# Rotary columns and the first branch's gate computed channel by token in a hybrid attention kernel

## The chip, the cores and the metric

The kernel runs on one core of a Trainium2 chip. The time is device microseconds of one execution: 505.21 us as the median of three (505.19 to 505.41). The profiled execution took 505.35 us; its span from the first to the last instruction is 503.6 us, and TensorE's granted clock was 0.998 of full speed over it.

## The reference, cut to what matters

One layer on 512 tokens of width 1024, in float32. All projections come from one matrix product of the normalised input:

```python
h = rmsnorm(x, norm_g)
(a_q, a_k, a_v, a_z, i_q, i_k, i_w, b_q, b_k, b_v, b_z, b_o, b_i, b_f, g_a, g_b) = split(h @ w_in)
q_a, k_a = rope(a_q), rope(a_k)             # 8 heads of 64; the first 16 of a head are rotated
q_i, k_i = rope(i_q), rope(i_k)             # 16 indexer heads of 64, one key head
score = sum_h w_i[h] * relu(q_i[h] @ k_i / 8)       # chunk-causal; the best 128 keys of each query stay
o_a = softmax(q_a @ k_a / 8 over those keys) @ v_a
y_a = (o_a * silu(a_z)) @ w_branch_a
q_b, k_b = silu(causal_conv(b_q, b_k))      # 4 taps, 4 heads of 128
cell = mlstm(q_b, k_b, b_v, log_i, log_f)
y_b = (head_norm(sigmoid(b_o) * cell) * silu(b_z)) @ w_branch_b
x = x + (sigmoid(g_a) * y_a + sigmoid(g_b) * y_b) @ w_out
return rmsnorm(x, final_norm_g)
```

The rotation takes partner channels c and c+8 of a head's first 16: x1*cos - x2*sin and x1*sin + x2*cos.

## The kernel before

Every large product is made of three matmuls of rounded parts: each operand is split into a rounded part (hi) and a remainder (lo), and hi*hi, hi*lo and lo*hi are added in PSUM (`three`, L1483). A weight slot holds 1024 columns; SP loads it into one of three raw buffers, ScalarE rounds it (`round_slot`, L868), POOL makes the remainder (`remainder`, L522), and seven split slots are kept.

TensorE's programme is written out by hand. It goes through UNITS: one small unit (indexer key, weights and gate logits), then the groups iq0, iq1, aq, ak, bq, bk, bv, av, bo, bz, az of 512 columns each. A unit is one PSUM bank (`pj`, two of them in turn) of 128 by 512, made of 24 matmuls in four quarters of six. Groups bq and bk have the weight columns as the stationary operand and so come out channel by token, with one unit for 128 channels; all others come out token by channel, with one unit for 128 tokens. iq0 and iq1 have three units each, since the first 128 tokens need no scores. After UNITS come eight rounds c, each with two gate units (g_a and g_b) and two branch products, and then the output projection.

Between the quarters stand side jobs, put at a place by `plan` (L112): place p is quarter p % 4 of unit p // 4. Every engine walks the same places and does its part of the job in order, so an engine that waits in one job holds back all that it has in later places. A job's PSUM comes from one of three rings of two banks (`tr`, `qb`, `ob`). The jobs that matter here:

- stage_chan (14 of them): a unit of iq0, iq1, aq or ak is copied by ScalarE to `stage`, VectorE rotates it with three operations on 128 columns (`rotate_from_bank`, L1135), TensorE turns it channel by token with four transposes, and ScalarE and VectorE split it into iq_parts or k_parts (aq goes to q_a unsplit).
- gate_rows, gate_cols: the mLSTM's gate logs are turned into rows, scanned, and turned back.
- score (48): two matmuls of a head's queries with the indexer keys, relu by ScalarE to `ob`, weighted sum by VectorE. The order is all heads of tokens 384 to 511, then 256 to 383, then 128 to 255.
- the top-k rounds (`round_plan`, L201): 16 rounds for each of three score blocks of 512, 384 and 256 columns, on VectorE alone.
- out_a_chan (4): the unit's gate tanh(a_z/2)+1 times a_z, multiplied with the inverse softmax sums (L1408), is turned by four transposes and multiplied into the attention output o_at (L1332), which is then split into oa_hi (L973) and oa_lo (L1345).

For bq and bk VectorE does the convolution from the unit's bank (`conv`, L1228) in three operations; TensorE may write that bank again, two units later, when the last of them is done (`wait_unit_read`, L578).

## Time and profile before

| | us |
|---|---|
| median of three runs | 505.21 |
| profiled execution | 505.35 |
| its span | 503.6 |
| TensorE busy | 494.5 (98%) |
| VectorE busy | 261.4 (52%) |
| ScalarE busy | 239.2 (47%) |
| POOL busy | 213.0 (42%) |

A busy TensorE counts matmuls that overlap: a row's duration of one matmul is longer than its distance from the next, so distances between starts are what a count of matmuls is multiplied with. Where the page gives a row of digits, each digit is a fortieth of the span, 12.6 us, in tenths of busy time. "Line engine" groups name what an operation writes and reads; `tr<-ident,stage` is a transpose.

### The profile page before, as it was taken

Reading aid. Unit: us, or ns where it says so; the run is one execution under the profiler, and the core shown is the slowest. Engines: PE = TensorE matmul, PEld = TensorE weight load, DVE = VectorE, ACT = ScalarE, POOL = GpSimd, SP = SyncE. Lnnn points to the kernel's source line nnn. Section 1 sums busy time; section 2 is a strip of 40 time slices with the busy share of each in tenths; the row PEclk is TensorE's granted clock in tenths of the full one; section 3 lists DMA queues with packets and bytes.
Section 4 is the critical chain, followed back from the end, with each engine's and each line's share of the span. In section 5 each row is a group of like instructions: output and inputs, shape, how many; then the busy total and the mean of one; then the engine's idle time right before and its main releaser. Section 6 shows DMA issues by size and latency. Waiting matters only on the chain.

```text
span 503.6 us, 6823 instructions
## 1 busy us (share of the span) xinstructions
PE 494.5 (98%) x2518; PEld 411.6 (82%) x2518; DVE 261.4 (52%) x575; ACT 239.2 (47%) x434; POOL 213.0 (42%) x130
## 2 busy tenths in 40 slices
PE   8999999999999999999999999999999999999995
PEld 7688888888888888888788888888888888887885
DVE  3865777877899936525655567531111011125433
ACT  6757655555554455536568652413330333152322
POOL 0675131333344444247487451246534663373000
PEclk9999999999999999999999999999999999999999
DMA  8654432212343243112223112043234426453111
GB/s 284 188 153 128 126 87 79 84 48 80 83 111 99 85 117 104 52 43 85 57 70 85 43 43 65 20 125 104 62 87 125 126 58 193 126 149 144 42 55 72
DMA packets 44841, 48.94 MB, mean 97 GB/s; under 512 B 4996, under 2 KB 30212, under 8 KB 44808
## 3 DMA queue, kind: packets, MB, share of 16 engines
q1 hardware_dynamic: 43944, 47.65, 32.3%
q10 hardware_dynamic: 864, 0.86, 0.5%
q8 instruction: 20, 0.33, 0.3%
q14 instruction: 13, 0.11, 0.1%
HBM read 46.40 MB, written 2.11 MB: 96 GB/s over the span
## 4 chain that ended last, share of the span: by engine, by line
PE 94%; DMA 2%; SPq 1%; POOL 1%; ACT 1%; DVE 1%; issue 1%; DVEq 0%
PE pj L1486 24%; PE pj L1487 24%; PE pj L1488 24%; DMA w_raw<-in_w_in 2%; PE ob L1617 2%; PE tr L1606 2%; PE qb L1554 2%; PE qb L1553 2%; PE ob L1487 1%; PE qb L1487 1%; PE ob L1488 1%; PE qb L1488 1%; PE ob L1486 1%; PE qb L1486 1%; PE tr L1541 1%; PE qb L1601 1%
## 5 line engine op out<-in xcount | busy, mean ns | idle before, releaser
L529 POOL TENSOR_TENSOR w_lo<-w_raw,w_hi 128x1024 fp32r<-128x1024 f32 x70 | 168.9, 2424 | 156.3 <-ACT w_hi L875 156.0
L1486 PE MATMUL pj<-w_hi,h_hi 128*128 128x512 f32 x272 | 109.6, 403 | 0.0
L1488 PE MATMUL pj<-w_hi,h_lo 128*128 128x512 f32 x272 | 106.5, 392 | 0.0
L1487 PE MATMUL pj<-w_lo,h_hi 128*128 128x512 f32 x272 | 106.4, 391 | 0.0
L1486 PE MATMUL pj<-h_hi,w_hi 128*128 128x512 f32 (+1 forms) x200 | 78.1, 390 | 1.0 <-DVE h_lo L1129 1.0
L875 ACT ACTIVATE w_hi<-w_raw 128x1024 fp32r<-128x1024 f32 (+1 forms) x72 | 73.5, 1045 | 9.8 <-DMA w_raw<-in_w_out 6.3
L1488 PE MATMUL pj<-h_hi,w_lo 128*128 128x512 f32 (+1 forms) x200 | 77.9, 389 | 0.0
L1487 PE MATMUL pj<-h_lo,w_hi 128*128 128x512 f32 (+1 forms) x200 | 77.8, 389 | 0.0
L1488 PEld LDWEIGHTS pj<-w_hi,h_lo 128*128 128x128 f32 x272 | 51.1, 188 | 11.4
L1486 PEld LDWEIGHTS pj<-w_hi,h_hi 128*128 128x128 f32 x272 | 51.2, 188 | 8.3 <-issue 0.2
L1487 PEld LDWEIGHTS pj<-w_lo,h_hi 128*128 128x128 f32 x272 | 51.3, 188 | 8.0
L1443 DVE TENSOR_TENSOR prod<-qb,sig 128x512 f32<-128x512 f32 x8 | 5.5, 690 | 77.2 <-PE qb L1488 77.2
L1486 PEld LDWEIGHTS pj<-h_hi,w_hi 128*128 128x128 f32 (+1 forms) x200 | 37.3, 186 | 9.4 <-issue 1.3
L1488 PEld LDWEIGHTS pj<-h_hi,w_lo 128*128 128x128 f32 (+1 forms) x200 | 37.3, 186 | 8.1
L1487 PEld LDWEIGHTS pj<-h_lo,w_hi 128*128 128x128 f32 (+1 forms) x200 | 37.3, 186 | 7.8
L840 POOL TENSOR_TENSOR m_lo<-prod,m_hi 128x512 fp32r<-128x512 f32 x8 | 10.6, 1330 | 60.5 <-ACT m_hi L1088 60.5
L1211 DVE SCALAR_TENSOR_TENSOR score<-ob,idx_w,score 128x512 f32<-128x512 f32 (+2 forms) x45 | 27.7, 616 | 11.5 <-ACT ob L921 8.8
L921 ACT ACTIVATE ob<-qb 128x512 f32<-128x512 f32 (+2 forms) x48 | 22.0, 476 | 16.7 <-PE qb L1554 11.7
L966 ACT ACTIVATE probs<-probs,neg_max 128x128 f32<-128x128 f32 (+3 forms) x32 | 18.0, 562 | 23.3 <-DVE neg_max L1306 23.1
L1088 ACT ACTIVATE m_hi<-prod 128x512 fp32r<-128x512 f32 x8 | 5.1, 632 | 47.3 <-DVE prod L1446 47.3
L1315 DVE COPY probs_t<-tr 128x128 f32<-128x128 f32 (+3 forms) x32 | 15.6, 489 | 22.6 <-PE tr L1606 22.6
L1223 DVE MAX8 top<-score 128x8 f32<-128x512 f32 (+2 forms) x48 | 26.7, 556 | 0.9
(216 smaller groups left out, 817.3 us busy)
## 6 DMA issues: line engine op xcount, KB each, us to landing
w_raw<-in_w_in SPq DMA_DIRECT2D x60, 512.0 KB, 3.6
w_raw<-in_w_out SPq DMA_DIRECT2D x5, 512.0 KB, 3.5
x_tok<-in_x SPq DMA_DIRECT2D x4, 512.0 KB, 5.3
w_raw<-in_w_branch_a SPq DMA_DIRECT2D x8, 256.0 KB, 2.9
w_raw<-in_w_branch_b SPq DMA_DIRECT2D x8, 256.0 KB, 3.3
x_again<-in_x SPq DMA_DIRECT2D x1, 2048.0 KB, 9.3
w_late<-in_w_out SPq DMA_DIRECT2D x3, 512.0 KB, 6.1
out<-y_norm SPq DMA_DIRECT2D x4, 320.0 KB, 2.3
```

Of the source, the lines that this page charges most:

```text
L529: eng.tensor_tensor(lo[:, 0:m], raw_slot(n)[:, 0:m], hi[:, 0:m].bitcast(F32), ALU.subtract).then_inc(lo_by_dve if n in DVE_SLOTS else lo_b ...
L840: pool.tensor_tensor(m_lo[:, c, :], prod[:, c % 2, 0, :], m_hi[:, c, :].bitcast(F32), ALU.subtract)\
L875: act.activation(split_slot(n)[0][:, 0:m], raw_slot(n)[:, 0:m], ACT.Copy).then_inc(hi_made, 1)
L921: act.activation(ob[s % RELUS][:, 0:w], bank_of(job)[:, 0:w], ACT.Relu, scale=float(IDX_DIM) ** -0.5).then_inc(relu_made, 1)
L966: act.activation(probs[:, s % 2, 0:w], probs[:, s % 2, 0:w], ACT.Exp, scale=-1.0, bias=neg_max[:, s:s + 1], accum_out=p_sum[:, s:s + 1])\
L1211: ins = dve.scalar_tensor_tensor(out=acc, in0=ob[s % RELUS][:, 0:w], scalar=wt, in1=acc, op0=ALU.mult, op1=ALU.add)
L1223: link(dve.max(top8[:, i, :], acc))
L1315: dve.tensor_copy(probs_t[:, s % QUAD, 0:w], bank_of(job)[:, 0:w]).then_inc(probs_t_made, 1)
L1486: pe.matmul(bank, a_hi, b_hi, start=first, stop=False)
L1487: pe.matmul(bank, a_hi, b_lo, start=False, stop=False)
L1488: return pe.matmul(bank, a_lo, b_hi, start=False, stop=last)
L1553: pe.matmul(bank[:, 0:w], queries, ik_hi[:, 0:w], start=True, stop=False)
```

## The change

Groups iq0, iq1, aq, ak and az now come out channel by token, like bq and bk: one unit for 128 channels and all tokens. iq0 and iq1 have four units each, with 384 columns (tokens 128 to 511). The transposes of stage_chan and out_a_chan are gone.

The rotation now has its partner in another row. When a group of four units is complete, ScalarE issues four transfers that copy rows 8 to 15 to rows 0 to 7 and back, for both heads of a block, into `swapped` ("swap"). POOL multiplies each block of `swapped` with the sines ("sin"), VectorE multiplies the block with the cosines and adds ("turn"), and ScalarE and VectorE split it ("parts"). The tables cos_t and sin_t, channel by token, are blank from memsets on POOL at the start and filled in the rotated rows by four ScalarE copies in gate_rows, whose four transposes now carry both gate logs and both tables. gate_cols has four transposes too.

Scores go head by head over the three token blocks, since a unit now carries all tokens of two heads, and start eight quarters after iq1 begins. The top-k rounds all start after the last score, one step of 4.5 quarters for a round of each block.

For az, the inverse softmax sums are taken in one operation after the last head ("recip"), turned by one transpose ("sums_chan"), copied, written to a scratch in HBM by a ScalarE transfer, and spread from there over the partitions by two SP transfers into rec_all. Four jobs "gate_a" scale the gate, multiply it into o_at, and split; the last two stand after the az units.

```diff
-UNITS = [("small", 0)] + [(g, j) for g in GROUPS for j in ((3, 2, 1) if g in ("iq0", "iq1") else range(TILES))]
+TURNED = ("iq0", "iq1", "aq", "ak")
+UNITS = [("small", 0)] + [(g, j) for g in GROUPS for j in range(TILES)]
...
-SCORES = [(i, h) for i in (3, 2, 1) for h in range(IDX_HEADS)]
+SCORES = [(i, h) for h in range(IDX_HEADS) for i in (3, 2, 1)]
...
 def score_place(s):
-    return first_quarter("iq1") + 4 + (4 * s) // 5
+    return first_quarter("iq1") + 8 + (4 * s) // 5
...
-    for n, u in enumerate(STAGED):
-        put(4 * UNIT[u] + 4 + 2, "stage_chan", n)
+    for n, g in enumerate(TURNED):
+        end = first[g] + 16
+        put(end, "swap", n)
+        for b in range(KW):
+            put(end + 4 + 3 * b, "sin", 4 * n + b)
+            put(end + 5 + 3 * b, "turn", 4 * n + b)
+            if (g, b) in PARTS:
+                put(end + 6 + 3 * b, "parts", PARTS.index((g, b)))
...
-        if j < TILES - 1:
-            put(first["az"] + 4 * j + 6, "out_a_chan", j)
+    put(first["az"] + 8, "recip")
+    put(first["az"] + 10, "sums_chan")
+    put(first["az"] + 14, "gate_a", 0)
+    put(first["az"] + 15, "gate_a", 1)
...
 def round_plan():
     at = {}
-    start = score_place(IDX_HEADS - 1) + 1
-    place = start
+    start = score_place(len(SCORES) - 1) + 1
     for r in range(ROUNDS):
+        place = start + (9 * r) // 2
         at.setdefault(place, []).append((3, r))
-        place += 4 if first_quarter("ak") <= place < first_quarter("bq") else 2
-    pairs = place
-    assert pairs > score_place(len(SCORES) - 1)
-    for r in range(ROUNDS):
-        at.setdefault(pairs + 3 * r, []).append((2, r))
-        at.setdefault(pairs + 3 * r, []).append((1, r))
+        at.setdefault(place + 2, []).append((2, r))
+        at.setdefault(place + 2, []).append((1, r))
...
@@ SP, after the load of slot GATE0 + 5
+                if n == GATE0 + 5:
+                    sp.wait_ge(rec_kept, 16)
+                    for e in range(2):
+                        half = rec_d[e * TILES * KW:(e + 1) * TILES * KW, :].rearrange("s t -> (s t)")
+                        sp.dma_start(rec_all[e * A_DIM:(e + 1) * A_DIM, :, :, :].rearrange("p i b t -> p (i b t)"),
+                                     half.partition_broadcast(A_DIM)).then_inc(rec_spread, 16)
...
@@ POOL
+            pool.memset(gate_l[:, :, :], 0.0)
+            pool.memset(two_rows[:, :], 0.0)
+            pool.memset(cos_t[:, :], 1.0)
+            pool.memset(sin_t[:, :], 0.0)
+            pool.memset(swapped[:, :], 0.0).then_inc(blank_made, 1)
...
+                    if job[0] == "sin":
+                        g, b = TURNED[job[1] // KW], job[1] % KW
+                        pool.wait_ge(rope_made, 4)
+                        pool.wait_ge(swap_in, 64 * (job[1] // KW + 1))
+                        pool.tensor_tensor(swapped_rows(g, b), swapped_rows(g, b), table(sin_t, g), ALU.mult)\
+                            .then_inc(sin_made, 1)
...
@@ ScalarE
+                elif kind == "swap":
+                    n = job[1]
+                    g = TURNED[n]
+                    size = KW * (SEQ - first_token(g))
+                    act.wait_ge(unit_out, UNIT[(g, KW - 1)] + 1)
+                    if n:
+                        act.wait_ge(rotated, KW * n)
+                    for first in (0, A_DIM):
+                        low, high = slice(first, first + HALF), slice(first + HALF, first + ROT)
+                        act.dma_start(swapped[low, 0:size], chan_flat(g)[high, :]).then_inc(swap_in, 16)
+                        act.dma_start(swapped[high, 0:size], chan_flat(g)[low, :]).then_inc(swap_in, 16)
+                elif kind == "parts":
+                    n = job[1]
+                    g, b = PARTS[n]
...
+                    act.wait_ge(rotated, KW * TURNED.index(g) + b + 1)
                     for e in range(2):
-                        src, hi, _ = part(job, e)
+                        src, hi, _ = part(n, e)
                         act.activation(hi, src, ACT.Copy).then_inc(part_hi_made, 1)
...
@@ VectorE
+                elif kind == "turn":
+                    m = job[1]
+                    g, b = TURNED[m // KW], m % KW
+                    rows_b = chan_rows(g, b)
+                    dve.wait_ge(rope_made, 4)
+                    dve.wait_ge(swap_in, 64 * (m // KW + 1))
+                    dve.tensor_tensor(rows_b, rows_b, table(cos_t, g), ALU.mult).then_inc(cos_made, 1)
+                    dve.wait_ge(cos_made, m + 1)
+                    dve.wait_ge(sin_made, m + 1)
+                    dve.tensor_tensor(rows_b, rows_b, swapped_rows(g, b), ALU.add).then_inc(rotated, 1)
...
+                elif kind == "gate_a":
+                    b = job[1]
+                    dve.wait_ge(zt_made, TILES + b + 1)
+                    dve.wait_ge(rec_spread, 32)
+                    gate = gate_a[:, (b + 2) % KW, :].rearrange("p (i t) -> p i t", t=P)
+                    dve.tensor_tensor(gate, gate, rec_all[:, :, b, :], ALU.mult).then_inc(gate_a_scaled, 1)
+                    dve.wait_ge(gate_a_scaled, b + 1)
+                    dve.wait_ge(o_at_made, TILES)
+                    dve.scalar_tensor_tensor(out=o_at[:, :, b, :], in0=gate, scalar=0.5, in1=o_at[:, :, b, :],
+                                             op0=ALU.mult, op1=ALU.mult).then_inc(oa_gated, 1)
+                    dve.wait_ge(oa_gated, b + 1)
+                    dve.wait_ge(o_hi, TILES + b + 1)
...
@@ TensorE
-                        if g in CHAN_GROUPS:
-                            a, b = w_part(n, c + j * P, c + (j + 1) * P), h_part(k, 0, SEQ)
+                        wide = SEQ - first_token(g)
+                        if g in CHAN_GROUPS + TURNED + ("az",):
+                            a, b = w_part(n, c + j * P, c + (j + 1) * P), h_part(k, SEQ - wide, SEQ)
                         else:
                             a, b = h_part(k, j * P, (j + 1) * P), w_part(n, c, c + WIDTH)
-                        ins = three(bank[:, :], a, b, k == 0, k == KT - 1)
+                        ins = three(bank[:, 0:wide], a, b, k == 0, k == KT - 1)
```

How instructions stand now, at three places. First VectorE in the kernel before, from the end of the convolution of the second bq unit to the start of that of the third (MAX and MATCH_REPLACE on `score` are a top-k round):

```order
L1234 SCALAR_TENSOR_TENSOR conv_acc<-pj,conv_w_col,conv_acc 128x511
L1223 MAX top_72<-score 128x8
L1224 MATCH_REPLACE score<-top_72,score 128x512
L1223 MAX top_72<-score 128x8
L1224 MATCH_REPLACE score<-top_72,score 128x512
L1226 TENSOR_SCALAR score<-score 128x512
L1234 SCALAR_TENSOR_TENSOR conv_acc<-pj,conv_w_col,conv_acc 128x509
```

VectorE in the changed kernel, from the end of the convolution of the second bq unit to the start of that of the third (`k_chan` with `cos_t` and `swapped` is a turn, `k_parts` a parts job):

```order
L1308 SCALAR_TENSOR_TENSOR conv_acc<-pj,conv_w_col,conv_acc 128x511
L1335 TENSOR_TENSOR k_chan<-k_chan,cos_t 128x512
L1338 TENSOR_TENSOR k_chan<-k_chan,swapped 128x512
L1344 TENSOR_TENSOR k_parts<-k_chan,k_parts 64x512 x2
L1297 MAX top_71<-score 128x8
L1298 MATCH_REPLACE score<-top_71,score 128x384
L1297 MAX top_71<-score 128x8
L1298 MATCH_REPLACE score<-top_71,score 128x256
L1335 TENSOR_TENSOR k_chan<-k_chan,cos_t 128x512
L1338 TENSOR_TENSOR k_chan<-k_chan,swapped 128x512
L1297 MAX top_71<-score 128x8
L1298 MATCH_REPLACE score<-top_71,score 128x512
```

Between the two convolutions two top-k rounds stood before; now two turns, a parts job and three rounds do.

ScalarE in the kernel before, around the end of iq1 (`ob<-qb` is the relu of a score):

```order
L921 ACTIVATE ob<-qb 128x512
L992 ACTIVATE stage<-pj 128x512
L921 ACTIVATE ob<-qb 128x512
L875 ACTIVATE w_hi<-w_raw 128x1024
L921 ACTIVATE ob<-qb 128x512 x3
L913 ACTIVATE iq_parts<-tr 64x4x128 x2
```

ScalarE in the changed kernel, from the last evacuation of iq1 to the first relus of aq:

```order
L1071 ACTIVATE iq_chan_112<-pj 128x384
L987 ACTIVATE iq_parts<-iq_chan_111 64x384 x2
L995 ACTIVATE ob<-qb 128x512
L933 ACTIVATE w_hi<-w_raw 128x1024
L977 DMA swapped<-iq_chan_112 8x1536
L978 DMA swapped<-iq_chan_112 8x1536
L977 DMA swapped<-iq_chan_112 8x1536
L978 DMA swapped<-iq_chan_112 8x1536
L995 ACTIVATE ob<-qb 128x384
```

The four transfer issues stand between a slot's rounding and the next relus.

VectorE in the changed kernel, around the first gate_a jobs (`gate_a<-gate_ring` takes the az unit out of its bank):

```order
L1473 SCALAR_TENSOR_TENSOR gate_a<-gate_ring_97,pj 128x512
L1417 TENSOR_TENSOR gate_a<-gate_a,rec_all 128x512
L1420 SCALAR_TENSOR_TENSOR o_at<-gate_a,o_at 128x4x128
L1425 TENSOR_TENSOR oa_lo<-o_at,oa_hi 128x512
L1417 TENSOR_TENSOR gate_a<-gate_a,rec_all 128x512
L1420 SCALAR_TENSOR_TENSOR o_at<-gate_a,o_at 128x4x128
L1425 TENSOR_TENSOR oa_lo<-o_at,oa_hi 128x512
L1473 SCALAR_TENSOR_TENSOR gate_a<-gate_ring_98,pj 128x512
L1417 TENSOR_TENSOR gate_a<-gate_a,rec_all 128x512
```

Two whole gate_a jobs stand ahead of the operation that frees the last az unit's bank.

## Rows read from the trace of the kernel before

**Rows 1.** The page: busy time of each engine, and VectorE in 40 slices.
```profile
PE 494.5 (98%) x2518; PEld 411.6 (82%) x2518; DVE 261.4 (52%) x575; ACT 239.2 (47%) x434; POOL 213.0 (42%) x130
...
DVE  3865777877899936525655567531111011125433
```

**Rows 2.** Waits of TensorE: who waited for whom, us, times, longest.
```profile
PE tr L1519 <- ACT small_chan L986: 0.2, 1, 0.2
```

**Rows 3.** Timeline of VectorE in bq and bk: start us, duration us, operation.
```profile
132.01 0.68 DVE L1223 MAX8 top<-score 128x8 f32<-128x512 f32 x1
...
133.52 0.69 DVE L1223 MAX8 top<-score 128x8 f32<-128x512 f32 x1
...
142.99 0.55 DVE L1223 MAX8 top<-score 128x8 f32<-128x384 f32 x1
...
145.22 2.31 DVE L1234 SCALAR_TENSOR_TENSOR conv_acc<-pj,conv_w_col,conv_acc 128x509 f32<-128x509 f32 x3
...
151.92 2.31 DVE L1234 SCALAR_TENSOR_TENSOR conv_acc<-pj,conv_w_col,conv_acc 128x509 f32<-128x509 f32 x3
```

**Rows 4.** Timeline of ScalarE at the second bk unit's end.
```profile
154.74 0.78 ACT L1000 ACTIVATE conv_acc<-pj,conv_b_col,conv_w_col 128x512 f32<-128x512 f32 x1 [3.19 <-PE pj L1488]
```

**Rows 5.** Timeline of TensorE in iq0 and at scores.
```profile
29.67 0.39 PE L1488 MATMUL pj<-w_hi,h_lo 128*128 128x512 f32 x1
29.90 0.60 PE L1541 MATMUL tr<-ident,stage 128*128 128x128 f32 x4
30.25 0.48 PE L1486 MATMUL pj<-w_hi,h_hi 128*128 128x512 f32 x1
30.57 0.39 PE L1487 MATMUL pj<-w_lo,h_hi 128*128 128x512 f32 x1
...
38.53 0.39 PE L1486 MATMUL pj<-w_hi,h_hi 128*128 128x512 f32 x1
...
42.39 0.39 PE L1488 MATMUL pj<-w_hi,h_lo 128*128 128x512 f32 x1
...
78.98 0.33 PE L1553 MATMUL qb<-ik_hi,iq_parts 128*128 128x384 f32 x1
...
79.69 0.40 PE L1486 MATMUL pj<-w_hi,h_hi 128*128 128x512 f32 x1
```

**Rows 6.** Groups by shape: busy us, mean ns of one, idle before and releaser.
```profile
L781 POOL CAST w_hi<-w_raw 128x1024 fp32r<-128x1024 f32 x2 | 2.1, 1042 | 10.8 <-DMA w_raw<-in_w_in 10.8
L758 POOL MEMSET q_lo<- 64x1024 f32 x2 | 1.9, 948 | 0.4 <-PE ob L1586 0.4
L875 ACT ACTIVATE w_hi<-w_raw 128x1024 fp32r<-128x1024 f32 x71 | 72.7, 1049 | 9.8 <-DMA w_raw<-in_w_out 6.3 <-PE pj L1488 1.6 <-DMA w_raw<-in_w_in 1.6
L828 POOL TENSOR_TENSOR gated<-gated,norm_b_row 128x512 f32<-128x512 f32 x4 | 5.2, 1289 | 7.7 <-DVE gated L1387 7.6
L1470 DVE TENSOR_TENSOR y_norm<-y_tok,final_row 128x512 f32<-128x512 f32 x7 | 4.8, 692 | 0.2
L973 ACT ACTIVATE oa_hi<-o_at 128x512 fp32r<-128x512 f32 x4 | 2.5, 628 | 11.9 <-DVE o_at L1332 11.9
L1488 PEld LDWEIGHTS pj<-w_hi,h_lo 128*128 128x128 f32 x272 | 51.1, 188 | 11.4
```

**Rows 7.** Timeline of SP's transfer issues.
```profile
50.65 1.89 SPq L708 DMA_DIRECT2D neg_m_all<-neg_m_d  x4
```

**Rows 8.** DMA issues: KB each, median us from issue to landing.
```profile
neg_m_all<-neg_m_d SPq DMA_DIRECT2D x4, 256.0 KB, 4.8
out<-y_norm ACTq DMA_DIRECT2D x4, 192.0 KB, 2.6
```

**Rows 9.** Timeline of POOL and of VectorE beside it, from 25 us.
```profile
25.90 7.13 POOL L529 TENSOR_TENSOR w_lo<-w_raw,w_hi 128x1024 fp32r<-128x1024 f32 x3 [3.15 <-ACT w_hi L875]
...
29.16 1.53 DVE L1177 TENSOR_TENSOR gate_l<-gate_l,gate_t 128x16 f32<-128x16 f32 x1
```

**Rows 10.** Tile oa_lo: duration ns min/median/max, first and last start.
```profile
L1345 DVE TENSOR_TENSOR oa_lo<-o_at,oa_hi x4: 682/2285/2895, 311.0 to 330.4; 128x512 fp32r<-128x512 f32 x4
```

**Rows 11.** Timeline of TensorE: transposes in az, first matmul of gates.
```profile
315.07 0.60 PE L1624 MATMUL tr<-ident,gated 128*128 128x128 f32 x4
...
322.81 0.39 PE L1486 MATMUL pj<-h_hi,w_hi 128*128 128x512 f32 x1
```

333 lines of the change are left out of this document (167 added, 166 removed).

## The prediction, made before the changed kernel was run

> **What bounds the kernel now.** I read the page first, then the waits of TensorE, then the timelines of single stretches. The page shows TensorE busy 98% of the span [rows 1], and of its waits those after the start, from the one for small_chan on, are 0.2 us [rows 2]. From 21 us on TensorE never stops, so a microsecond of its work removed is a microsecond gained, and a wait put in front of it is one lost. The second thing to see is VectorE: in slices 11 to 13 of 40 (138 to 176 us) it is at 9 tenths [rows 1]. There it runs the convolutions of "bq" and "bk", whose PSUM banks TensorE needs two units later, and between them the top-k rounds. The bank of the first "bk" unit is read by the convolution at 151.92 us, which ends at 154.24. ScalarE takes up the second "bk" unit at 154.74, released by TensorE 0.1 to 0.2 us earlier, so TensorE starts the third, in the first one's bank, at 154.6 [rows 3, 4]. VectorE is 0.4 us early: a queue that is nearly the bound without a wait to show it.
>
> **TensorE's own work.** A matmul of 512 columns comes every 0.227 us (17 steps from 38.53 to 42.39), one of 384 every 0.177 (4 steps, 78.98 to 79.69) [rows 5]. Four transposes make the step from 29.67 to 30.57 us 0.90 where two plain ones are 0.455: 0.445 us a group [rows 5].
> - Gone: 14 groups of stage_chan (56 transposes) and 4 of out_a_chan: 18 x 0.445 = 8.0 us.
> - gate_rows and gate_cols go from eight transposes to four each, about 0.4 us each: 0.8. sums_chan adds one transpose, 0.2.
> - iq0 and iq1: 144 matmuls of 512 columns become 192 of 384. The first six run before TensorE waits for small_chan at 20.8 us in either kernel [rows 2], so 138 x 0.227 = 31.3 becomes 186 x 0.175 = 32.6 (0.175 to 0.177 by the rows): +1.2.
> - az, aq and ak swap the operands' roles at the same size: nothing.
> Net -7.4 us. The profiled execution took 505.35 (505.21 is the median, 0.1 less), so with every wait hidden the time would be 497.9.
>
> **Start.** Five memsets on POOL, 4,096 columns in all. Two of 1024 columns take 0.95 us each, so about 3.8 us; POOL idles 10.8 us there until its first slot lands [rows 6]. Nothing; if the cover were gone it would cost at most 3.8.
>
> **Place 1, iq1 (VectorE, ScalarE, POOL and the new transfers).** Before, a rotated unit waited for one PE pass; now a group of four must be whole, then: ScalarE issues four swaps, they land, POOL multiplies by sin, VectorE by cos and adds, ScalarE and VectorE split, TensorE scores. Call t the end of iq0 on TensorE. ScalarE empties the bank (0.5), rounds slot 9 (1.05, [rows 6]) and issues four transfers at 0.47 each (1.89 for four on SP, [rows 7]): t+3.4. A transfer of 192 KB issued by ScalarE landed 2.6 us after its issue, SP's neg_m_all of 256 KB 4.8 [rows 8]; a swap is 48 KB, so I take 2.6, with 4.8 as the upper end and, being smaller, 1 us less as the lower: t+6. POOL has the remainder of slot 10 ahead of sin_0, and ScalarE rounds that slot only after the first iq1 unit (24 x 0.175 = 4.2, plus evacuation and 1.05: t+5.8), so POOL is free at t+8.2 (2.38 a remainder, [rows 9]). sin_0 of 384 columns takes 1.0 (1.29 for 512, [rows 6]); the cos product may slip in ahead of it (0.6): sin done t+9.7, add 0.6, two roundings 1.0, the last remainder 0.6: t+12. TensorE is at score 0 after 54 matmuls and gate_cols: 54 x 0.175 + 0.445 = t+9.9. It waits 2 us. Behind it, ScalarE stands in "parts" waiting for VectorE's turn while relus of scores queue after it, and then four transfer issues (1.9) and a slot rounding (1.05) stand ahead of the relus in the first aq unit; with two score banks TensorE has about 2.4 us of scores ahead. I take 1 us for each of the three parts jobs and swaps that fall among scores. Place 1: 5 us. Bounds: 2 if only the first wait stays, 8 if each of the later holds is twice as long. In aq and ak the quarters are 1.8 us and VectorE has room.
>
> **Place 2, bq and bk (VectorE).** This term carries the forecast. What went away for VectorE there is one k_parts pair; what comes is large. Step prices: a 512-wide top-k round 1.51 us (132.01 to 133.52), a 384+256 pair 2.23 (142.99 to 145.22), a convolution 2.23 to the next start, three steps of 2.32 in all [rows 3]; a 512-column product or sum of two SBUF tiles 0.69, with the gap 0.72 [rows 6]. A turn is two such, 1.44, and a parts job two on 64 partitions, which I price alike. Per unit of the new order:
> - bq0: pair, round, convolution
> - bq1: pair, turn, parts, round = 6.6, then convolution: 8.9
> - bq2: turn, parts, pair, turn, round = 8.1: 10.3
> - bq3: parts, pair, turn, parts = 6.6: 8.8
> - bk0 to bk3: round and pair = 3.7: 6.0 each
> TensorE needs 24 x 0.227 = 5.46 a unit. Let bq0 start at 0. Its convolution must wait for the unit and ScalarE: 6.5 to 8.7. Then the convolutions end at 17.6, 27.9, 36.7, 42.7, 48.7, 54.7, 60.7, and a unit starts not before the convolution two units back: bq3 at 17.7 instead of 16.4, bk0 at 28.0 (after 23.2, 4.8 lost), bk1 at 36.8 (3.3 lost), then each waits 0.5 more, and the second bv unit starts at 60.8 instead of 49.1: 11.7 us lost. All this is work that the old order did elsewhere or not at all: the 512-wide rounds now start at the end of ak instead of in aq (ten of them were done by bq), and turns and remainders cost 11.5 us that small rotations of 128 columns did not. Where VectorE waits there for a swap or for sin, it has the backlog to hide it.
> The new operations have both operands in SBUF, and such ones are stretched while POOL works: a subtraction of 16 columns took 1.53 us inside POOL's run from 25.90 to 33.03 [rows 9], and oa_lo took 0.68 at best and 2.90 at worst [rows 10]. About eight POOL instructions (four sin, four remainders) fall in this stretch and VectorE is in such operations 11.5 of some 28 us: 8 x 0.41 x 1 us (half a remainder is 1.2, half a sin 0.6) = 3; turned down to 2, since POOL runs ahead while VectorE is late. The Trainium skill, page "SBUF — State Buffer", section "SBUF: two separate sides", says that the vector engine and GpSimd share one port pair as an exclusive lock, which a vector instruction with two SBUF inputs needs against a GpSimd one that reads SBUF. By that rule, the trace agrees (0.68 against 2.90 us), and it speaks against this change: all 32 new turn operations and the remainders, which used to read PSUM, come under it. Without it the 2 us would be 0, with every encounter at its worst it is the third rival.
> Place 2: 13.7. Bounds: 9.8, if the eight turn and parts jobs take 1.2 us each instead of 1.44, and 20, if each of the eight POOL instructions costs VectorE a full microsecond.
>
> **Place 3, az and the first gate units.** Before, the az gates went through PE token by token. Now all reciprocals go out together after the last head: one transpose where 315.07 stands [rows 11], a copy 0.4, issue 0.4, 2.6 to HBM, two SP issues 0.9, and the spread, 4.8 by neg_m_all's landing [rows 8]: at 324.0 (bounds 321.5 and 327; twice the bytes per transfer, half as many). VectorE stands at gate_a 0 and 1 with the last az unit's bank behind them. Each gate_a is three operations of 0.69 with a ScalarE copy of 0.63 between [rows 6], 3.0 with gaps: two end at 330.0, the az bank is free at 330.7. TensorE ends the first gate unit at 322.8 - 0.9 + 0.2 + 5.5 = 327.6 [rows 11] (its old start, two transpose groups less since 315, one transpose more, 24 matmuls) and needs that bank: 3.1 lost. gate_a 2 and 3 then end at 336.7, with three POOL remainders beside them about 338.5 (oa_lo already took a median of 2.29, [rows 10]); TensorE is at the branch matmuls at 336.2: 2.3 more. Place 3: 5.4; bounds 0 (spread 3 us early, lock absent) and 9.
>
> **Sum.** 505.35 - 7.4 + 5 + 13.7 + 5.4 = 522.0. Lowest corner 509.8, highest 535.
>
> **Rivals.**
> - A, only place 2 binds (VectorE as the bound in bq/bk, no lock; swaps and the reciprocal spread hidden). For it: my landings are medians, and scores can be served late by two banks. Against: 2 us at score 0 comes out of plain durations. 505.35 - 7.4 + 11.7 = 509.7.
> - B, the other side: TensorE's saving is kept, 498. It decides if VectorE keeps pace, that is if the turn and parts jobs (11.5 of the 11.7 us) hide in gaps of VectorE that I don't see. For it: the page shows no wait of TensorE for VectorE, and VectorE is busy 52% over the span [rows 1]. Against it: the 0.4 us of slack [rows 3, 4].
> - C, the lock decides: each POOL instruction in places 1 to 3 (about 20) blocks a VectorE operation for 1 us: +11 more, 533. For it oa_lo's 2.9; against, POOL is busy 42% of the span [rows 1].
> - D, the change does not do what it says: 384 columns come at the pace of the weight load, 0.188 us by its duration [rows 6]; 186 x 0.013 = +2.4, 524. Against: 0.177 in [rows 5].
>
> **Chances.** Forecast (all three places stall, 514 to 530) 0.62; A 0.16; C 0.11; B 0.06; D 0.03; 0.02 for a result within 0.2% of before, where savings and stalls cancel. Range 508 to 532. What a measurement of this kernel tells from no change is about 0.2%, 1 us: faster 0.07, same 0.02, slower 0.91.
>
> **What would show it.** TensorE idle that is new: at the first score for iq_parts by VectorE, in bq to the first bv unit for the convolution on VectorE (over 9 us in all), before the second gate unit and before the first branch for VectorE's az chain. VectorE at 9 tenths over the whole of bq and bk, convolutions ending about 11 us later than TensorE's pace allows. 384-column matmuls 0.175 apart. turn operations at 0.69 and some above 1.5. If VectorE shows no backlog in bq, the forecast is wrong at its largest term; if rec_all lands before az ends, place 3 is.

## The result and the profile after

The changed kernel takes 541.04 us (median of 4 runs, 539.15 to 542.10) against 505.20 us (505.16 to 505.41) for the kernel before: ratio 1.0704, 95% interval 1.0674 to 1.0734. Forecast were 522.0, within 508 to 532. The direction is right, the size is not: the slowdown is 35.8 us in place of 16.8. The line numbers below are those of the changed kernel unless another kernel is named.

The page of the changed kernel: busy time of each engine, then VectorE and TensorE's granted clock in 40 slices, to be held against [rows 1].

```profile
PE 500.8 (93%) x2487; PEld 417.0 (77%) x2487; DVE 291.8 (54%) x567; ACT 241.4 (45%) x441; POOL 238.9 (44%) x151
...
DVE  4735949689999995568764555183011111025343
...
PEclk9999999999977899999999999987999999999998
```

TensorE fell from 98% to 93% of its span. VectorE has 30 us more to do and stands at 9 tenths in six slices in a row in place of three (9 to 14 counted from 0, 122 to 203 us). New is the last row: in slices 11 to 13 (149 to 189 us) and 26, 27 the granted clock is at 7 to 8 tenths; before, its mean was 0.998 and only the last slice was lower (0.93; 0.90 now). The longest waits of TensorE answer to [rows 2] (behind the start there were three before, of 0.2 us each, of which [rows 2] show one); the columns are us in all, times, longest:

```profile
PE pj L1562 <- DVE conv_acc L1308: 15.0, 4, 6.5
PE qb L1619 <- ACT ob L995: 4.8, 6, 2.0
PE qb L1562 <- DVE oa_lo L1425: 3.9, 1, 3.9
PE pj L1562 <- DVE gate_a L1473: 2.9, 1, 2.9
PE qb L1619 <- DVE iq_parts L1344: 2.7, 1, 2.7
```

All the places that were forecast are there, the convolutions (place 2), the scores (place 1) and the chain of az (place 3), and behind the start nothing else over 0.5 us. From the distances between TensorE's starts: 31.6 us more of standing still, 11.5 us more in matmuls that come at 0.43 us instead of 0.227, and, as the span grew by 36.6 (503.6 to 540.2), 6.5 us less work of its own.

Place 2 on VectorE, for [rows 3]: start, duration, operation.

```profile
125.95 2.89 DVE L1335 TENSOR_TENSOR q_a<-q_a,cos_t 128x512 f32<-128x512 f32 x1
128.88 2.91 DVE L1338 TENSOR_TENSOR q_a<-q_a,swapped 128x512 f32<-128x512 f32 x1
...
136.97 2.32 DVE L1308 SCALAR_TENSOR_TENSOR conv_acc<-pj,conv_w_col,conv_acc 128x509 f32<-128x509 f32 x3
...
146.56 2.32 DVE L1308 SCALAR_TENSOR_TENSOR conv_acc<-pj,conv_w_col,conv_acc 128x509 f32<-128x509 f32 x3
148.79 2.12 DVE L1335 TENSOR_TENSOR k_chan<-k_chan,cos_t 128x512 f32<-128x512 f32 x1
150.94 1.66 DVE L1338 TENSOR_TENSOR k_chan<-k_chan,swapped 128x512 f32<-128x512 f32 x1
...
160.13 2.32 DVE L1308 SCALAR_TENSOR_TENSOR conv_acc<-pj,conv_w_col,conv_acc 128x509 f32<-128x509 f32 x3
```

The last turn of aq takes 5.8 us where two operations of 0.69 were priced. So VectorE enters bq 4.4 us late, before anything of bq's own. The convolutions start 9.6 and 13.6 us apart; TensorE produces a unit every 5.46. And POOL in the same stretch:

```profile
125.89 2.40 POOL L556 TENSOR_TENSOR w_lo<-w_raw,w_hi 128x1024 fp32r<-128x1024 f32 x1 [4.58 <-ACT w_hi L933]
128.85 2.39 POOL L556 TENSOR_TENSOR w_lo<-w_raw,w_hi 128x1024 fp32r<-128x1024 f32 x1 [0.56 <-ACT w_hi L933]
```

The product with cos starts 0.06 us behind one slot remainder and is done 0.5 us behind its end; the sum does the same with the next. A VectorE operation of 0.69 us is held here (it can't end before POOL's instruction does) and takes 2.9. The same can be read at all 18 operations of turns and parts that took over 0.3 us too long: each started while a POOL instruction ran and ended 0.4 us (384 columns) or 0.5 to 0.6 us (512) behind the end of it. Five that started 0.02 to 0.5 us ahead of a remainder took their usual 0.55 or 0.69. Both can be seen at one remainder, VectorE's two operations first:

```profile
115.42 0.68 DVE L1335 TENSOR_TENSOR q_a<-q_a,cos_t 128x512 f32<-128x512 f32 x1
116.14 2.76 DVE L1338 TENSOR_TENSOR q_a<-q_a,swapped 128x512 f32<-128x512 f32 x1
```

```profile
115.77 2.59 POOL L556 TENSOR_TENSOR w_lo<-w_raw,w_hi 128x1024 fp32r<-128x1024 f32 x1 [2.80 <-ACT w_hi L933]
```

Place 3 shows the same, in the second pair of az gates, for [rows 10]; POOL's row covers three remainders:

```profile
356.57 7.97 POOL L556 TENSOR_TENSOR w_lo<-w_raw,w_hi 128x1024 fp32r<-128x1024 f32 x3 [17.75 <-ACT w_hi L933]
```

```profile
356.85 2.64 DVE L1417 TENSOR_TENSOR gate_a<-gate_a,rec_all 128x512 f32<-128x512 f32 x1
359.53 2.77 DVE L1420 SCALAR_TENSOR_TENSOR o_at<-gate_a,o_at 128x512 f32<-128x512 f32 x1
363.07 2.03 DVE L1425 TENSOR_TENSOR oa_lo<-o_at,oa_hi 128x512 fp32r<-128x512 f32 x1 [0.77 <-ACT oa_hi L1051]
365.02 0.68 DVE L1417 TENSOR_TENSOR gate_a<-gate_a,rec_all 128x512 f32<-128x512 f32 x1
```

And TensorE behind the last of its waits there, for [rows 11]:

```profile
368.03 0.76 PE L1562 MATMUL qb<-oa_hi,w_hi 128*128 128x512 f32 x1 [3.88 <-DVE oa_lo L1425]
...
369.02 0.63 PE L1564 MATMUL qb<-oa_hi,w_lo 128*128 128x512 f32 x1
369.44 0.63 PE L1562 MATMUL qb<-oa_hi,w_hi 128*128 128x512 f32 x1
...
374.17 0.39 PE L1562 MATMUL ob<-ob_hi,w_hi 128*128 128x512 f32 x1
374.40 0.39 PE L1563 MATMUL ob<-ob_lo,w_hi 128*128 128x512 f32 x1
```

Each takes 0.63 us and they start 0.43 apart, until at 374 they are back at 0.39 and 0.23. The windows say what that is; the columns are busy time of PE, PEld, DVE, ACT and POOL with counts, the granted clock, the DMA share and GB/s:

```profile
156.00:170.00 14.00, 7.15 (x25) 5.46 (x24) 12.73 (x24) 4.41 (x7) 2.36 (x1) 0.76 0.13 37
...
195.00:350.00 155.00, 154.82 (x921) 129.29 (x921) 91.29 (x256) 83.43 (x189) 73.95 (x58) 1.00 0.26 74
350.00:375.00 25.00, 18.27 (x62) 14.12 (x61) 14.70 (x14) 8.22 (x11) 7.97 (x3) 0.80 0.23 63
```

Behind the waits of 2.9 to 6.5 us, and behind the one of 2.0 us at 66 us, the clock granted to TensorE is for some 3 to 6 us the lower of its two levels, 1.2 instead of 2.4 GHz; behind the one of 2.7 us at 50 us it stays at the higher, and where TensorE never stops it is 1.00.

### The profile page after: what moved, and what is told of

Read it like the earlier page. It is cut to its first block, busy times and chain, and to the rows that moved or that the text cites. A ratio compares the mean times of both kernels' runs of the same rounds, so it can differ in the third digit from the quotient of the medians.

```text
span 540.2 us, 6826 instructions
## 1 busy us (share of the span) xinstructions
PE 500.8 (93%) x2487; PEld 417.0 (77%) x2487; DVE 291.8 (54%) x567; ACT 241.4 (45%) x441; POOL 238.9 (44%) x151
## 4 chain that ended last, share of the span: by engine, by line
PE 65%; DVE 15%; issue 8%; DMA 3%; POOL 3%; ACT 3%; SPq 1%; ACTq 0%; DVEq 0%; POOLq 0%
PE pj L1562 16%; PE pj L1564 16%; PE pj L1563 16%; DMA w_raw<-in_w_in 2%; PE ob L1683 2%; PE tr L1672 2%; POOL w_lo L556 2%; PE qb L1562 2%; DVE conv_acc L1308 2%; POOL swapped L826 1%; PE qb L1564 1%; PE qb L1563 1%; PE ob L1562 1%; DVE score L1298 1%; PE ob L1564 1%
## 5 line engine op out<-in xcount | busy, mean ns | idle before, releaser
L1562 PE MATMUL pj<-h_hi,w_hi 128*128 128x512 f32 (+2 forms) x360 | 142.2, 395 | 18.9 <-DVE conv_acc L1308 15.0
L1563 PE MATMUL pj<-h_lo,w_hi 128*128 128x512 f32 (+2 forms) x360 | 139.9, 389 | 0.0
L1564 PE MATMUL pj<-h_hi,w_lo 128*128 128x512 f32 (+2 forms) x360 | 139.8, 388 | 0.0
L1562 PEld LDWEIGHTS pj<-h_hi,w_hi 128*128 128x128 f32 (+1 forms) x360 | 69.4, 193 | 33.3 <-DVE conv_acc L1308 16.6
L1564 PEld LDWEIGHTS pj<-h_hi,w_lo 128*128 128x128 f32 (+1 forms) x360 | 69.2, 192 | 13.1
L1563 PEld LDWEIGHTS pj<-h_lo,w_hi 128*128 128x128 f32 (+1 forms) x360 | 69.6, 193 | 11.5
L1562 PE MATMUL pj<-w_hi,h_hi 128*128 128x512 f32 x128 | 51.8, 405 | 0.0
L1564 PE MATMUL pj<-w_hi,h_lo 128*128 128x512 f32 x128 | 50.1, 392 | 0.0
L1563 PE MATMUL pj<-w_lo,h_hi 128*128 128x512 f32 x128 | 50.0, 391 | 0.0
L898 POOL TENSOR_TENSOR m_lo<-prod,m_hi 128x512 fp32r<-128x512 f32 x8 | 10.7, 1332 | 65.0 <-ACT m_hi L1171 65.0
L1285 DVE SCALAR_TENSOR_TENSOR score<-ob,idx_w,score 128x512 f32<-128x512 f32 (+2 forms) x45 | 27.7, 616 | 12.3 <-ACT ob L995 10.1
L1563 PEld LDWEIGHTS pj<-w_lo,h_hi 128*128 128x128 f32 x128 | 24.1, 189 | 3.7
```

The lines of the kernel that those rows point to most:

```text
L1285: ins = dve.scalar_tensor_tensor(out=acc, in0=ob[s % RELUS][:, 0:w], scalar=wt, in1=acc, op0=ALU.mult, op1=ALU.add)
L1562: pe.matmul(bank, a_hi, b_hi, start=first, stop=False)
L1563: pe.matmul(bank, a_hi, b_lo, start=False, stop=False)
L1564: return pe.matmul(bank, a_lo, b_hi, start=False, stop=last)
```

## The experiments

Every kernel was timed beside the kernel before on the same chip (505.0 to 505.4 us). Where not said otherwise, the whole computation is done.

### Who holds VectorE

**Turns with one operand in PSUM.** Line 1335 and 1338 read a PSUM bank for their second operand; the rotation is therefore not computed.

```diff
-  dve.tensor_tensor(rows_b, rows_b, table(cos_t, g), ALU.mult)
+  other = table(bank_of(("gate_rows",)), g)
+  dve.tensor_tensor(rows_b, rows_b, other, ALU.mult)
...
-  dve.tensor_tensor(rows_b, rows_b, swapped_rows(g, b), ALU.add)
+  dve.tensor_tensor(rows_b, rows_b, other, ALU.add)
```

> The changed kernel with the turns' second operand (cos, then the swapped rows) read from a PSUM bank in place of SBUF; POOL's products with sin, the swaps and all waits stay. So the rotation is not computed, but the same number of instructions of the same shape run. Theory 1 (VectorE with two SBUF operands is held while POOL works: the turns average 1.4 to 2.0 us in aq and 1.0 in ak): the turns fall to about 0.7 us each, VectorE's busy time falls by 15 us or so, of which place 1 and the front of place 2 give 4 to 8 us of time, 533 to 537. Theory 2 (the long turns are long for another reason, or the parts jobs and remainders, which still have two SBUF operands, take over the delay): VectorE's busy time falls by under 5 us, time 539 to 541.

528.45 us (ratio 1.0456, 1.0434 to 1.0479): 12.6 us less, in the direction of theory 1 and more than its 4 to 8. Every turn operation took 0.55 us (384 columns) or 0.69 (512). The parts jobs of the same kernel, which kept two SBUF operands, were still stretched, by 5.7 us in 8 operations.

**The same with the full computation.** cos is copied once into a free PSUM bank, the product goes to a second, the swapped rows are added there, the parts are taken from there.

```diff
+  act.activation(tr[0][:, :], cos_t[:, :], ACT.Copy)
...
-  dve.tensor_tensor(rows_b, rows_b, table(cos_t, g), ALU.mult)
+  dve.tensor_tensor(turned, rows_b, table(tr[0], g), ALU.mult)      # turned = tr[1]
-  dve.tensor_tensor(rows_b, rows_b, swapped_rows(g, b), ALU.add)
+  dve.tensor_tensor(rows_b if g == "aq" else turned, turned, swapped_rows(g, b), ALU.add)
```

> The changed kernel, with the full computation, in which no turn or parts operation of VectorE has two operands in SBUF: the table of cos is copied once to a free PSUM bank (0.5 us on ScalarE), the product with cos is written to a second free PSUM bank, the swapped rows are added there, and the two parts are taken from there. The kernel that only read stand-ins from PSUM in the turns gained 12.6 us, but it did not rotate. Theory 1 (VectorE's operations with two SBUF operands are held by POOL, nothing else): turns 0.55 to 0.7 us each, parts 0.45 to 0.6 instead of 0.73 to 0.84, time 541 - 12.6 - 2 = 526.5, 524 to 529. Theory 2 (the stand-in kernel gained because something else of the rotation was left out): 535 or more.

525.09 us (1.0397, 1.0380 to 1.0414): 15.9 us less than the changed kernel, theory 1. Groups of equal shape, busy us and mean ns, first of the changed kernel, then of this one:

```profile
L1338 DVE TENSOR_TENSOR q_a<-q_a,swapped 128x512 f32<-128x512 f32 x4 | 8.1, 2016 | 1.4 <-POOL swapped L826 1.3
...
L1335 DVE TENSOR_TENSOR q_a<-q_a,cos_t 128x512 f32<-128x512 f32 x4 | 5.5, 1383 | 0.0
```

```profile
L1346 DVE TENSOR_TENSOR q_a<-tr,swapped 128x512 f32<-128x512 f32 x4 | 2.8, 692 | 1.5 <-POOL swapped L827 1.4
L1343 DVE TENSOR_TENSOR tr<-q_a,tr 128x512 f32<-128x512 f32 x4 | 2.8, 688 | 0.1
```

Same shapes and, for the sum, the same swapped rows from SBUF; with one operand in PSUM none is stretched. Operation by operation in the changed kernel, 18 of the 56 turn and parts operations were stretched by over 0.3 us, 21.1 us in all: 9.4 in iq, 8.1 in aq, 3.6 in ak. Here 34 of the 56 run beside a POOL instruction and none is stretched by more than 0.02 us. The Trainium skill, page "SBUF — State Buffer", section "SBUF: two separate sides", has the rule that the forecast weighed: of a VectorE operation with two SBUF inputs and a GpSimd one that reads SBUF, the one that starts first keeps the shared ports for its whole instruction and the other stands still. The two kernels agree with it: held were only those operations that started behind POOL's (18 of 18), and none with an operand in PSUM.

**Without POOL's 16 products with sin** (the swapped rows are added as they are, so the rotation is not computed).

```diff
-  pool.tensor_tensor(swapped_rows(g, b), swapped_rows(g, b), table(sin_t, g), ALU.mult)
-  dve.wait_ge(sin_made, m + 1)
```

> The changed kernel without POOL's 16 products with sin (the swapped rows are added as they are, so the rotation is not computed); swaps, turns and everything else as changed, VectorE's operations keep two SBUF operands. It leaves POOL 22 us of work less; of what may hold VectorE only POOL's remainders of the weight slots stay. Theory 1 (each POOL instruction that meets such an operation holds it, the remainders most, since they are 2.4 us each): of the 16.0 us that the form through PSUM gave, the sin products held at most 16 operations for about half of 1.3 us, and VectorE also waited 5 us for sin: time 541 - 6 to 9, 532 to 535; the turns fall to 0.8 to 1.2 us on average. Theory 2 (the sin products, which stand right beside the turns, are the holders): turns at 0.7 us, 525 to 528. Theory 3 (the hold needs neither): 539 or more.

532.18 us (1.0519, 1.0501 to 1.0537): 8.9 less, theory 1. Part of that is that VectorE no longer waits for the products; the runs don't separate it. Ten operations are still stretched, by 13.6 us together, four of them by 2.1 to 2.2 us each, and all ten beside a remainder. So the remainders of 2.4 us, which POOL always did, hold more than the new sin products; the change brought the operations that can be held.

### What the lower clock costs

**Useless matmuls in front of place 2's waits**, so that TensorE is not idle.

```diff
+  FILL = {('bq', 3): 16, ('bk', 0): 26, ('bk', 1): 13}
+  for _ in range(FILL[(g, j)]):
+      pe.matmul(qb[0][:, :], h_hi[:, 0, 0:P], h_hi[:, 0, :], start=True, stop=True)
```

> The changed kernel with useless matmuls of 512 columns (their result is overwritten) on TensorE ahead of three waits of place 2: 16 before the fourth bq unit, 26 before the first bk unit, 13 before the second, about as long as the waits of 4.0, 6.6 and 3.5 us there. Nothing else differs and the results are the same. Theory 1 (an idle TensorE is then granted a lower clock, and the steps of 0.43 us a matmul instead of 0.227 behind each wait are a cost of their own, 5.6 us in place 2): the granted clock stays near 1.0 from 145 to 180 us, the 0.43 steps there are gone, and the time falls by about 4 to 5 us, to 536.5. Theory 2 (the clock falls for another reason, or VectorE sets the pace of place 2 whatever TensorE does): the time stays at 541 or grows by what the dummies exceed the waits, 1 to 2 us. Theory 3 (the slow matmuls lie in time in which VectorE is still late, so they cost nothing): clock back, time the same.

539.72 us (1.0693, 1.0668 to 1.0718; the changed kernel 1.0674 to 1.0734). The slow matmuls of place 2 went from 5.6 us to 1.5 in the trace, and the time moved by no more than the intervals allow: theory 3. VectorE sets the pace there: its first convolutions start 9.59, 13.57 and 10.49 us apart in the changed kernel and 9.59, 13.63 and 10.49 here. Slow matmuls only fill time in which TensorE would have waited longer.

**The same in front of place 3's waits** (11 and 16 matmuls).

> The changed kernel with useless matmuls of 512 columns (overwritten later, results the same) ahead of the two waits of place 3: 11 before the second gate unit (2.5 us at 0.227, the wait was 3.0) and 16 before the first branch matmul (3.6 us, the wait 4.0). Behind these waits 7 and 13 matmuls came 0.43 us apart, 4.2 us over their full pace. In place 2 the same edit brought the clock back and gave only about 0.6 us, since VectorE was late there anyway. Here TensorE is its own bound behind the waits. Theory 1 (behind a wait the lower clock is a cost of its own wherever nothing else is late): the 0.43 steps are gone and 3 to 4 us of time with them, 537.3. Theory 2 (what follows is late for another reason, or the clock falls anyway): 540.5 to 541.5.

539.08 us (1.0665, 1.0645 to 1.0685), between the theories; the interval still touches that of the changed kernel, so only the traces tell what was gained. The rows behind the last wait:

```profile
366.32 0.50 PE L1562 MATMUL qb<-oa_hi,w_hi 128*128 128x512 f32 x1 [1.60 <-DVE oa_lo L1425]
366.65 0.39 PE L1563 MATMUL qb<-oa_lo,w_hi 128*128 128x512 f32 x1
```

At full pace from the second on. From the first to the twelfth it takes 2.64 us, where the kernel with fillers in place 2 alone took 4.18 (365.90 to 370.08): 1.5 us, less 0.4 because rec_all landed 0.4 us later in this execution. Up to the first gate unit the two traces are within 0.2 us. The slow matmuls between the two waits cost nothing: the first branch matmul starts 11.0 us behind the second gate unit's first in all three kernels, by VectorE's chain. Of the 11.5 us in slow matmuls only those behind the last wait of a place count, and only where nothing else is late: 1.5 us by the fillers to 2.7 by the changed kernel's own rows here, and 1.3 in place 1 (last section), which was not tested by fillers.

### Moving work without removing it

**Top-k rounds from aq, ak and bq into bk, bv and av.**

```diff
-  start = score_place(len(SCORES) - 1) + 1
+  start = first_quarter("bk")
-      place = start + (9 * r) // 2
+      place = start + (31 * r) // 8
```

> The changed kernel with the 32 top-k rounds moved: they start with the bk group instead of in aq and ak and stand 31/8 quarters of a unit apart, so that none stands in bq. Theory 1 (the rounds, moved into bq and bk by the change, make VectorE's backlog there together with the turns): the waits of TensorE for the convolutions, 15.6 us, and the slow matmuls behind them, 5.6, fall to under 4 us together, time about 523 to 525. Theory 2 (the turns, the parts jobs and the delays from POOL alone are as long as VectorE can bear): half of it stays, 531. Theory 3 (the rounds now fill VectorE in bk and bv as they did in bq): the wait moves there, 536 to 541.

540.64 us (1.0712, 1.0682 to 1.0743): nothing, theory 3. The waits for convolutions fell from 15.0 to 9.6 us, and 4.2 us came at the first masked softmaxes, whose masks were now late. Even with no round in bq, TensorE waited 3.5 and 2.4 us for bq's convolutions: turns and parts were enough.

**All scores one unit later.**

> The changed kernel with all 24 scores one unit (4 quarters) later, and the rounds behind them 35/8 quarters apart in place of 9/2. Theory 1 (place 1 waits because the first score stands too close behind the last iq1 turn): the wait of 2.9 us at the first score goes, and of the 5.9 us of later ones the half, time -4 to -5, 536.5. Theory 2 (VectorE is simply late from iq1 to bk and every microsecond given back at the scores is waited for in bq): place 1 falls, place 2 rises by the same, 540 to 542.

543.32 us (1.0750, 1.0734 to 1.0766), 2.3 more: theory 2, and worse. The first wait of 2.7 us went; one of 5.2 us for ScalarE stood at 54 to 59.2 us instead.

### The first branch's gate

**As before the change, all else as changed.**

> The changed kernel with the first branch's gate as it was before the change: token by channel units, gates scaled token-major and transposed on TensorE (four groups of four transposes, 1.8 us, less the one transpose of the sums), no sums in HBM; the rotated columns stay as changed. Theory 1 (place 3 costs 7.1 us of waits and 4.2 us of slow matmuls behind them): 541.0 - 11.3 + 1.6 = 531.4. Theory 2 (only the waits belong to it; the clock falls there anyway): 535.6. Theory 3 (the old form waits as well, since place 2 has made everything behind it late): above 538.

531.90 us (1.0527, 1.0511 to 1.0543): 9.1 less, theory 1 (531.4). No wait and no slow matmul is left behind 310 us.

**With the turns through PSUM.**

> Both edits together, full computation: turns and parts through PSUM banks, and the first branch's gate token by channel as before the change (which alone gave 531.9, 9.1 less). Theory 1 (the delay by POOL and place 3 are separate costs): 526.5 - 9.1 = 517.4, 515 to 520. Theory 2 (they overlap, since place 3 is late only because place 2 is): 522 or more.

516.93 us (1.0228, 1.0203 to 1.0253): 8.2 less than the turns through PSUM alone, theory 1. The two costs add, to within 1 us.

### Can the change be made to pay?

**Turns of ak 6 quarters apart, rounds spread over bq to av**, on the last kernel.

> The kernel with turns and parts through PSUM and the gate of the first branch as before (516.9), with VectorE's remaining work spread: the four ak turns 6 quarters apart instead of 3, so over bq and bk, and of the 16 top-k rounds 3 in bq, 3 in bk, 5 in bv, 4 in av. In the kernel it starts from, TensorE waits 8.7 us in bq for the convolutions, 1.6 us in small steps up to bv, and 2.9 us lie in slow matmuls. Per unit VectorE then has convolution 2.32, half a turn and parts pair 1.4, and 0.4 of a round 1.5: 5.3 against TensorE's 5.46. Theory 1 (place 2 without the delay by POOL is only a matter of where the work stands): 516.9 minus 8 to 12, 505 to 509, at or just above the kernel before the change. Theory 2 (VectorE is full over the whole stretch from iq1 to av): the waits move to bv and av, 513 or more.

516.72 us (1.0224, 1.0210 to 1.0238): theory 2. The waits of 8.1 us in bq and bk became 4.8, and 5.4 us came for masks at 241 to 248 us.

**The same with scores 2 quarters later.**

> As the kernel with the work spread, and all scores 2 quarters later, for the 1.8 us that TensorE waits at the first score. Theory 1: 1.8 us less than that kernel. Theory 2 (as when the scores went 4 quarters later in the changed kernel, +2.3 us): the scores then run into the swaps and turns of aq on ScalarE, and the wait comes back there: the same or 1 to 2 us more.

515.95 us (1.0223, 1.0200 to 1.0246), no difference that can be told.

**Last 8 heads tile by tile**, so that the widest tile's rounds can start in ak. The places of the rounds and of the ak turns move with it (not shown); the second kernel has fewer rounds in ak, bq and bk.

```diff
-SCORES = [(i, h) for h in range(IDX_HEADS) for i in (3, 2, 1)]
+SCORES = [(i, h) for h in range(8) for i in (3, 2, 1)] + [(i, h) for i in (3, 2, 1) for h in range(8, IDX_HEADS)]
```

> Base as in the kernel with the work spread (turns and parts through PSUM, the first branch's gate as before, ak turns over bq and bk; 516.7). New: the scores of the last 8 heads are taken token tile by token tile, so that the widest tile's 16 scores are complete 12 scores earlier, and 8 of its 16 top-k rounds (1.5 us each) stand in ak, where VectorE is idle for 7 us in pieces; two rounds' worth less stands in bq and bk, and the last one ends before attention begins. Theory 1 (VectorE has too much work between the end of the scores and the start of attention, about 4 us more than the 97 us it has there, and room before): the waits of 5.1 us in bq and bk, of 5.7 us at the first masked softmaxes, and the slow matmuls behind them fall to 2 to 4 us together: 506 to 509. Theory 2 (VectorE is as full in ak as after it, or its lateness holds the scores): 513 or more.

> As the kernel before it, with 6 rounds in ak instead of 8, one pair of rounds fewer in bq and bk (3 turns' distance kept), more in bv and av. Theory 1: places 1 and 2 wait less than in that kernel, the last masks come late by up to 3 us: the same time within 2 us. Theory 2 (only the load in ak, bq and bk decides): 1 to 3 us less than that kernel.

509.41 (1.0082, 1.0068 to 1.0096) and 508.67 us (1.0065, 1.0051 to 1.0079). Theory 1 of the first, 0.4 us above its 506 to 509: VectorE was overfull behind the scores and had room before them. The second came out as its theory 1, within 2 us of the first, and 0.7 less. What is left are heads of its queue that are not ready. VectorE in the second of these kernels:

```profile
130.86 0.70 DVE L1334 TENSOR_TENSOR tr<-k_chan,tr 128x512 f32<-128x512 f32 x1 [2.23 <-DMA swapped<-k_chan]
132.20 0.70 DVE L1337 TENSOR_TENSOR tr<-tr,swapped 128x512 f32<-128x512 f32 x1 [0.65 <-POOL swapped L823]
133.62 1.41 DVE L1344 TENSOR_TENSOR k_parts<-tr,k_parts 64x512 fp32r<-64x512 f32 x2 [0.72 <-ACT k_parts L987]
```

3.6 us of standing still in one turn, with the convolution behind it.

**Turns of ak 2 to 9 quarters later, parts two behind, rounds in the gaps; then all scores one quarter later.**

```diff
-  at_sin, at_turn, at_parts = ((4, 6, 7), (9, 11, 13), (15, 17, 19), (21, 23, 25))[b] if g == "ak" else ...
+  at_sin, at_turn, at_parts = ((6, 8, 10), (14, 16, 18), (22, 24, 26), (28, 32, 34))[b] if g == "ak" else ...
```

> Base: scores tile by tile for the last 8 heads, turns and parts through PSUM, first branch's gate as before (508.7). There VectorE stands 2.2 us at the first ak turn for the swapped rows, 0.7 for sin and 0.7 for ScalarE's rounding, while TensorE waits 2.4, 0.9 and 0.8 us for the convolutions behind. New: the four ak turns stand 2 to 8 quarters later, each parts job two quarters behind its turn, and rounds fill the place (two of the widest in bq0 and bq1). Theory 1 (these waits are VectorE's queue standing at a head that isn't ready, not its load): the three waits of 4.1 us fall to under 1, time 505 to 506, level with the kernel before the change. Theory 2 (VectorE's load is the limit): the wait moves into bv or to the first masked softmaxes, 508 to 510.

> As the kernel with the ak turns later, and all scores one quarter later, for the 1.9 us that TensorE waits at the first score and the 0.7 at 91 us. Theory 1 (the first scores alone wait there): 1 to 1.4 us less than that kernel, 504 to 505. Theory 2 (later scores run into the aq turns): the same.

504.10 us (0.9984, 0.9973 to 0.9994) and 503.98 us (0.9972, 0.9961 to 0.9983). The first is theory 1 and 1 us better than its 505 to 506; nine of its twelve runs took 503.8 to 504.4 us, three 505.9 to 506.2. Between the two no difference can be told, which is theory 2 of the second. The second is faster than both kernels, by 1.4 us (0.3%) than the one before. Its page and its longest waits for VectorE and ScalarE behind the start:

```profile
PE 490.2 (98%) x2502; PEld 411.6 (82%) x2502; DVE 272.9 (54%) x570; ACT 241.2 (48%) x441; POOL 233.8 (47%) x151
```

```profile
PE qb L1623 <- ACT ob L995: 0.9, 2, 0.7
PE ob L1653 <- issue: 0.9, 1, 0.9
...
PE qb L1623 <- DVE iq_parts L1344: 0.6, 1, 0.6
```

## Why the prediction was wrong, step by step

- **TensorE's own work, -7.4.** Right: 6.5 less. Matmuls of 384 columns start 0.17 to 0.18 us apart (71.54 to 71.89 below), so the fourth rival falls.

```profile
71.54 0.33 PE L1619 MATMUL qb<-ik_hi,iq_parts 128*128 128x384 f32 x1
71.71 0.34 PE L1620 MATMUL qb<-ik_lo,iq_parts 128*128 128x384 f32 x1
71.89 0.40 PE L1562 MATMUL pj<-h_hi,w_hi 128*128 128x512 f32 x1
```

- **Start, 0.** Right: POOL still idled 7.0 us until its first slot landed.
- **Place 1, +5.** The first wait was sized well, 2.7 us for 2. The rest was not: 4.8 us of waits followed at the later scores where 3 were given. With turns and parts through PSUM all that follows is gone and the first is 1.8. The reason of the forecast, ScalarE's four transfer issues and slot roundings ahead of the relus, is not what held the scores; those issues (0.63 us each, not 0.47) are still there. It was the turns and parts in iq, stretched by 9.4 us. That the total lies within its bounds (7.5 us of waits, bounds 2 and 8) is luck in so far as the reason given for the later ones was the wrong one. Here they are at the first score, VectorE, POOL and TensorE in turn:

```profile
44.77 1.48 DVE L1335 TENSOR_TENSOR iq_chan<-iq_chan,cos_t 128x384 f32<-128x384 f32 x1 [1.22 <-DMA swapped<-iq_chan]
45.79 2.29 POOL L826 TENSOR_TENSOR swapped<-swapped,sin_t 128x384 f32<-128x384 f32 x2
...
47.23 1.27 DVE L1338 TENSOR_TENSOR iq_chan<-iq_chan,swapped 128x384 f32<-128x384 f32 x1 [0.98 <-POOL swapped L826]
...
50.37 0.47 PE L1619 MATMUL qb<-ik_hi,iq_parts 128*128 128x512 f32 x1 [2.68 <-DVE iq_parts L1344]
```

- **"In aq and ak the quarters are 1.8 us and VectorE has room." This is the step that failed,** together with the 2 us given for the hold by POOL in place 2 and in no other place. The forecast took the rule for bq and bk, counted eight POOL instructions there at 0.41 x 1 us, and priced nothing in iq and aq. Of 21.1 us of stretching 17.5 lay there. The two stretched operations at 125.95 and 128.88 alone delay VectorE's entry into bq by 4.4 us, and TensorE loses 5.1 us inside bq, where the forecast had 1.3. A hold is not a fixed 1 us either but all that is left of POOL's instruction: at 125.95 and 128.88, where VectorE started just behind a remainder, 2.2 us over 0.69. The term measured 15.9 us of time (kernel with turns through PSUM), against 2. The third rival had the mechanism and took 13 for it, 533 in all, still 8 short; it got 0.11. The first rival, place 2 alone, falls with the waits of places 1 and 3.
- **Place 2, 11.7 without the hold.** The arithmetic of VectorE's queue holds: through PSUM the waits there are 2.1, 5.3, 1.1 and four of 0.4, 10.1 us. That stalls in it ("it has the backlog to hide it") cost nothing is true while it is late and false at its edge: the repaired kernel gained 4.6 us from a standing queue head.
- **Place 3, +5.4.** The first wait is 2.9 us for 3.1, by durations that were all nearly right (reciprocals out, spread and landed in 9.1 us for 8.9). The second is 3.9 for 2.3: three operations of the third gate were held for 5.4 us where 1.8 were given. No run takes that hold away, so what it alone costs stays open. With the clock behind it the place costs 9.1 (the old gate's gain, with 1.6 us of transposes to pay for it: 10.7).
- **The clock** stood nowhere in the sum. It is a real term but small: by the fillers and rows 1.5 to 2.7 us in place 3, nothing that can be told in place 2, 1.3 in place 1. The 11.5 us that the rows show are not its price, since among waits a slow matmul only shortens the next one.
- **Sum.** Without any hold the forecast was 520.0. The kernel with turns and parts through PSUM has 525.1: TensorE's own work 0.9 us more than forecast, place 1 3.0 less, the waits of place 2 1.6 less and of place 3 1.5 more, and 5.8 us in slow matmuls in the two, which makes 523.6. Of the last 1.5, 0.5 is the distance from its profiled execution (524.6) to its median; the rest is not found in single rows. The hold, 15.9, gives 541.0.

That B, the saving kept, was given little was right for this order of the work, but some of the saving was there to be had: 1.4 us of the 5.8 that the rotated columns alone save (7.4 less 1.6 for the first branch's transposes, which that kernel keeps), with the hold removed and the queue reordered.

## What to carry to other kernels

An operation with two SBUF operands on VectorE is priced with all that POOL may do beside it, wherever in the program it stands and not only where VectorE is the bound: a lateness made in a slack place is carried to the tight one. Give such an operation one operand in PSUM if a bank is free; that alone was worth 15.9 us here. By the two runs with fillers, slow matmuls behind a wait are charged only behind the last wait of a place, where TensorE and nothing else sets the pace. And moving work on a queue that is full over the whole stretch moves the wait; look for the data dependency (here the order of scores) that lets it start earlier.
